# A trunk of two layers in one kernel: splits and reciprocals reordered in each layer's first up unit, loads and splits reordered at the start of the down products

## What is computed

```python
def conv_ffn(xn, buf, w_up, conv_w, conv_b, w_down):
    u = xn @ w_up
    g, v = u[..., :D_FF], u[..., D_FF:]
    gc, new_buf = causal_dwconv(g, buf, conv_w, conv_b)
    return (jax.nn.gelu(gc) * v) @ w_down, new_buf.astype(buf.dtype)
...
for layer in range(DEPTH):
    ...
    x = x + y
    f, f_i = conv_ffn(rmsnorm(x, P['f_norm'][layer]), ffn_conv[layer], P['f_w_up'][layer],
                      P['f_conv_w'][layer], P['f_conv_b'][layer], P['f_w_down'][layer])
    x = x + f
```

## Time and profile before

| | us |
|---|---|
| median of 3 runs | 2373.31 (2372.86 to 2375.99) |
| the profiled execution, its own time | 2375.29 |
| span of its trace | 2373.4 |
| TensorE busy | 2309.8 |
| VectorE busy | 1651.6 |
| ScalarE busy | 1012.8 |
| GpSimd busy | 1106.0 |
| mean granted TensorE clock | 0.987 |

### The profile page before, as it was taken

One profiled execution on the slowest core, in us unless ns is written; L12 is line 12 of the kernel. 1 busy time (PEld: TensorE's weight loads), 2 busy tenths in 40 slices (PEclk: granted clock), 3 DMA queues, 4 the chain that ended last, 5 costly groups with the idle time before them and its releaser, 6 DMA issues.

```text
span 2373.4 us, 43151 instructions
## 1 busy us (share of the span) xinstructions
PE 2309.8 (97%) x16883; PEld 2250.0 (95%) x16883; DVE 1651.6 (70%) x2170; ACT 1012.8 (43%) x1724; POOL 1106.0 (47%) x922
## 2 busy tenths in 40 slices
PE   9999997999999998999999999979999999989999
PEld 8999997999999998999999867979999999989999
DVE  7666547777777768886466675477777777788863
ACT  6555644333333334333344585443333333343331
POOL 3211454555555556556220253645555555465450
PEclk9999999999999999999999999999999999999999
DMA  4111121222222334312373203312222223243232
GB/s 132 45 45 44 61 95 52 76 81 81 81 71 65 110 115 155 110 62 96 119 108 86 65 10 107 102 50 82 81 72 64 82 81 106 84 165 112 78 101 89
DMA packets 228790, 203.04 MB, mean 86 GB/s; under 512 B 28373, under 2 KB 209821, under 8 KB 228412
## 3 DMA queue, kind: packets, MB, share of 16 engines
q1 hardware_dynamic: 224180, 188.87, 25.8%
q10 hardware_dynamic: 4404, 12.28, 2.1%
q0 software_dynamic: 64, 0.05, 0.0%
HBM read 152.41 MB, written 50.66 MB: 86 GB/s over the span
## 4 chain that ended last, share of the span: by engine, by line
PE 84%; DVE 7%; issue 4%; DMA 2%; ACT 1%; POOL 1%; SPq 0%; ACTq 0%; DVEq 0%; POOLq 0%
PE ps L1442 13%; PE ps L1441 13%; PE ps L1443 13%; PE ps L1216 9%; PE ps L1218 9%; PE ps L1217 9%; PE ps L1461 4%; PE ps L1462 4%; PE ps L1463 3%; PE ps L1676 1%; PE ps L1704 1%; PE ps L1728 1%; DVE later_slots L2944 1%; DMA part<-h_spill 1%; DVE ring L2950 1%
## 5 line engine op out<-in xcount | busy, mean ns | idle before, releaser
L1461 PE MATMUL ps<-ring,later_slots 128*128 128x272 f32 x960 | 279.6, 291 | 9.0 <-DVE later_slots L2944 9.0
L1462 PE MATMUL ps<-ring,later_slots 128*128 128x272 f32 x960 | 278.0, 290 | 0.0
L1463 PE MATMUL ps<-ring,later_slots 128*128 128x272 f32 x960 | 276.2, 288 | 0.0
L2922 DVE SCALAR_TENSOR_TENSOR y<-convin,fcol,y 128x1024 f32<-128x1024 f32 x192 | 224.4, 1209 | 18.5 <-ACT y L2147 16.8
L1441 PE MATMUL ps<-b,slot_a 128*128 128x272 f32 x768 | 221.1, 288 | 0.8 <-DVE slot_a L2876 0.8
L1442 PE MATMUL ps<-b,slot_a 128*128 128x272 f32 x768 | 221.3, 288 | 0.0
L1443 PE MATMUL ps<-b,slot_a 128*128 128x272 f32 x768 | 220.5, 287 | 0.0
L1461 PEld LDWEIGHTS ps<-ring,later_slots 128*128 128x128 f32 x960 | 182.3, 190 | 10.9 <-DVE later_slots L2944 10.8
L1462 PEld LDWEIGHTS ps<-ring,later_slots 128*128 128x128 f32 x960 | 183.0, 191 | 0.0
L1463 PEld LDWEIGHTS ps<-ring,later_slots 128*128 128x128 f32 x960 | 183.0, 191 | 0.0
L1216 PE MATMUL ps<-sa,whi 128*128 128x384 f32 (+1 forms) x540 | 178.0, 330 | 0.4 <-DVE x L2981 0.3
(11 more groups left out here) (493 smaller groups left out, 7925.0 us busy)
## 6 DMA issues: line engine op xcount, KB each, us to landing
rawu<-in_f_w_up SPq DMA_DIRECT2D x192, 256.0 KB, 4.3
h_spill<-x SPq DMA_DIRECT2D x48, 544.0 KB, 3.2
down_raw<-in_f_w_down SPq DMA_DIRECT2D x48, 384.0 KB, 4.4
part<-h_spill SPq DMA_DIRECT2D x30, 544.0 KB, 5.0
f_spill<-x ACTq DMA_DIRECT2D x16, 544.0 KB, 2.7
x<-f_spill SPq DMA_DIRECT2D x16, 544.0 KB, 7.2
raw<-in_a_w_in SPq DMA_DIRECT2D x16, 512.0 KB, 4.0
last_rows<-h_spill SPq DMA_DIRECT2D x12, 544.0 KB, 4.8
```

The lines of the kernel that those rows point to most:

```text
L1461: pe.matmul(out, slot[:, 0, i, :], b_hi, start=(i == 0 and not more), stop=False, skip_group_check=more)
L1462: pe.matmul(out, slot[:, 0, i, :], b_lo, start=False, stop=False, skip_group_check=more)
L1463: last = pe.matmul(out, slot[:, 1, i, :], b_hi, start=False, stop=(i == 2), skip_group_check=more)
L2922: ins = dve.scalar_tensor_tensor(out, g, fcol[:, u, col + t:col + t + 1], out, ALU.mult, ALU.add)
```

## The change

In the first unit of each layer: B22 and T2 are split in three rows and one as before (the piece is now called "three"), T3 and T4 in one row (2), two rows ("two") and one row (3), with row 2 of T4 and of T3 first, straight after T2's weights. Unit 1's rows are asked for when T3's row 2 is split. Reciprocal 0 moves from behind slot_b's second split to ahead of slot_c's first; reciprocal 1 moves from there to behind the last split of the unit; make_u2 moves ahead of slot_d's split and of reciprocals 1 and 2. ScalarE does slot_c's first part ahead of B22, and its third root after T4 instead of before T3. In the down products: down_raw[2] and down_raw[3] change places, stages 3 to 5 are issued before the loads of groups 2 and 3, these go half by half, and step 2's and 3's high parts wait for their first half alone. VectorE's split of B21 moves into q = 1, behind the split of the weights of step 3. The combos T3 and T4 of block 0 and B11, B21, T1 of block 1 move to later steps. No arithmetic is added or left out.

```diff
-        down_raw = [at(f"down_raw{p}", [P, 2, 3, 2, P], F32, reg_w + p * 12 * P * 4) for p in range(4)]
+        down_raw = [at(f"down_raw{p}", [P, 2, 3, 2, P], F32, reg_w + r * 12 * P * 4) for p, r in enumerate((0, 1, 3, 2))]
...
-        COMBO_ORDER += [("B11", 3), ("T1", 3), ("B22", "all"), ("B21", 3), ("B22", 3), ("T2", "all"), ("T2", 3),
-                        ("T3", "all"), ("T3", 3), ("T4", "all"), ("T4", 3)]
+        COMBO_ORDER += [("B11", 3), ("T1", 3), ("B22", "three"), ("B21", 3), ("B22", 3), ("T2", "three"), ("T2", 3),
+                        ("T4", 2), ("T3", 2), ("T3", "two"), ("T3", 3), ("T4", "two"), ("T4", 3)]
+        SPAN = {"three": 3, "two": 2}
...
                 elif u == 1:
-                    eng.wait_ge(c_lo, combo_at(layer, "T4", "all"))
+                    eng.wait_ge(c_lo, combo_at(layer, "T3", 2))
...
-                def pair_load(b, p):
...
-                        eng.wait_ge(w_lo, products_of(layer, gl) if p < 2 else ups_done(layer))
-                        eng.wait_ge(s_made, sums_of(layer, gl) if p < 2 else sums_of(layer, gl + 1))
+                        eng.wait_ge(w_lo, ups_done(layer) if p == 2 else products_of(layer, gl))
+                        eng.wait_ge(s_made, sums_of(layer, gl + 1) if p == 2 else sums_of(layer, gl))
                         if p > 0:
-                            eng.wait_ge(prod, products_of(layer, gl) + (0, 4, 6, 5)[p])
+                            eng.wait_ge(prod, products_of(layer, gl) + (0, 4, 5, 6)[p])
                     if b > 0 or p > 1:
-                        eng.wait_ge(unit_raw[p % 2], down_raw_in(layer, b, p) - 32)
+                        eng.wait_ge(unit_raw[p % 2], down_raw_in(layer, b, p) - (16 if parts == (1,) else 32))
...
-                    for e in range(2):
+                    for e in parts:
...
                 pair_load(0, 1)
-                stage(3)
-                pair_load(0, 3)
-                pair_load(0, 2)
-                stage(4)
-                stage(5)
+                for tt in range(3, FB):
+                    stage(tt)
+                for e in range(2):
+                    for p in (2, 3):
+                        pair_load(0, p, (e,))
...
-                    act.wait_ge(unit_raw[p % 2], down_raw_in(layer, b, p))
+                    act.wait_ge(unit_raw[p % 2], down_raw_in(layer, b, p) - (16 if (b, j) == (0, 0) and p > 1 else 0))
...
-                combo_hi(layer, "B22", "all")
                 weight_hi(layer, 0, 2)
+                combo_hi(layer, "B22", "three")
                 product_copy(layer, 0, 0)
                 weight_hi(layer, 0, 3)
                 scale(KD - 1)
                 combo_hi(layer, "B21", 3)
                 product_copy(layer, 0, 1)
                 combo_hi(layer, "B22", 3)
-                combo_hi(layer, "T2", "all")
+                combo_hi(layer, "T2", "three")
                 combo_hi(layer, "T2", 3)
                 weight_hi(layer, 0, 4)
+                combo_hi(layer, "T4", 2)
+                combo_hi(layer, "T3", 2)
                 root(v, 1)
-                root(v, 2)
-                combo_hi(layer, "T3", "all")
+                combo_hi(layer, "T3", "two")
                 combo_hi(layer, "T3", 3)
                 weight_hi(layer, 0, 5)
-                combo_hi(layer, "T4", "all")
+                combo_hi(layer, "T4", "two")
                 combo_hi(layer, "T4", 3)
+                root(v, 2)
                 weight_hi(layer, 0, 6)
                 weight_hi(layer, 1, 0)
...
-                    name_at = {4: "T1", 6: "B22", 11: "T2", 12: "T3", 16: "T4"}
-                    if q in name_at:
-                        down_combo_hi(layer, 0, name_at[q])
-                    elif q == 18:
-                        down_combo_hi(layer, 1, "B11")
-                    elif q < 20:
-                        pass
+                    early_ones = {4: (0, "T1"), 6: (0, "B22"), 11: (0, "T2"), 14: (0, "T3"), 18: (0, "T4"), 20: (1, "B11"),
+                                  25: (1, "B21"), 27: (1, "T1")}
+                    if q < NQ:
+                        if q in early_ones:
+                            down_combo_hi(layer, *early_ones[q])
...
-                combo_lo(layer, "B22", "all")
+                recip(v, 0)
                 weight_lo(layer, 0, 2)
+                combo_lo(layer, "B22", "three")
                 weight_lo(layer, 0, 3)
                 combo_lo(layer, "B21", 3)
                 combo_lo(layer, "B22", 3)
-                combo_lo(layer, "T2", "all")
+                combo_lo(layer, "T2", "three")
                 combo_lo(layer, "T2", 3)
                 weight_lo(layer, 0, 4)
-                recip(v, 0)
-                recip(v, 1)
-                combo_lo(layer, "T3", "all")
+                combo_lo(layer, "T4", 2)
+                combo_lo(layer, "T3", 2)
+                combo_lo(layer, "T3", "two")
                 combo_lo(layer, "T3", 3)
                 weight_lo(layer, 0, 5)
+                combo_lo(layer, "T4", "two")
+                combo_lo(layer, "T4", 3)
+                make_u2(layer, 0)
+                weight_lo(layer, 0, 6)
+                recip(v, 1)
                 seq.settle()
                 take_c11(layer, 0)
-                combo_lo(layer, "T4", "all")
-                combo_lo(layer, "T4", 3)
-                weight_lo(layer, 0, 6)
                 recip(v, 2)
-                make_u2(layer, 0)
                 seq.settle()
                 make_c12(layer, 0)
                 weight_lo(layer, 1, 0)
...
-                down_combo_lo(layer, 0, "B21")
...
-                    if q < 20:
-                        if q in (5, 7, 12, 13, 17, 19):
-                            name, to = {5: ("T1", 0), 7: ("B22", 0), 12: ("T2", 0), 13: ("T3", 0), 17: ("T4", 0),
-                                        19: ("B11", 1)}[q]
-                            down_combo_lo(layer, to, name)
-                        if q in (9, 15):
+                    early_ones = {1: (0, "B21"), 5: (0, "T1"), 7: (0, "B22"), 12: (0, "T2"), 15: (0, "T3"), 19: (0, "T4"),
+                                  21: (1, "B11"), 26: (1, "B21"), 28: (1, "T1")}
+                    if q <= NQ:
+                        if q in early_ones:
+                            down_combo_lo(layer, *early_ones[q])
+                        if q in (9, 17):
                             down_combo_make(layer, 0, "T2" if q == 9 else "T4")
```

More of the change, by code:

```diff
@@ L1471, in before @@
                     def before(cc, i):
-                        if cc == 0 and i == 0 and name in ("B22", "T2", "T3", "T4"):
-                            pe.wait_ge(c_lo, combo_at(layer, name, "all"))
+                        if cc == 0 and i == 0 and name in ("B22", "T2"):
+                            pe.wait_ge(c_lo, combo_at(layer, name, "three"))
+                        elif cc == 0 and i == 0 and name in ("T3", "T4"):
+                            pe.wait_ge(c_lo, combo_at(layer, name, "two"))
                         elif cc == 0 and i == 0 and name == "B21":
@@ L2119, in weight_hi @@
                 elif u == 0 and j == 6:
-                    act.wait_ge(c_lo, combo_at(layer, "T4", "all"))
+                    act.wait_ge(c_lo, combo_at(layer, "T4", "two"))
                 else:
```

9 lines of the change are left out of this document (5 added, 4 removed).

## The result

The changed kernel takes 2342.6 us, median of four runs (2340.2 to 2344.9), against 2373.8 (2372.9 to 2376.0) beside it: ratio 0.9867, interval 0.985 to 0.9884, so 31.2 us faster. Forecast were 2337.3 and a range of 2329 to 2351. The profiled execution took 2340.4 us with a span of 2338.2, 35.2 less than before's span.

The account below looks back on a forecast made before the run. TensorE is the path except in gaps, mostly behind VectorE's first_slots, slot_c and later_slots. First units 14.5 plus down products 23.2 make 37.7, less 1.7 gives 36.0: 2373.3 to 2337.3 us, range 2329 to 2351.

Parts of the forecast that it names:

- First unit of layer 0: Up to unit 1's product B21: finer splits and moved reciprocals start it at 401.1 instead of 407.56, gain 6.5 us.
- First unit of layer 1: Same code and waits as layer 0: 6.5 us, plus 1.5 for the half-speed stretch at 1600.4.
- Down products to step 4: Start of down products, a step being one weight group p of one product: step 4 at 898.4, gain 5.9 us.
- From step 4 on: Down products after step 4: the 5.9 us gained there counted in full in each layer's 11.6.
- The tables: Combos moved to later steps: 0.8 us of later_slots, 3.4 of two late waits, 1.5 of half-speed stretch, per layer.
- The crowding: VectorE's three-row work at steps 26 to 30: lag 2.9 us against some 3.2 of lookahead, so no cost.
- The allowance of 1.7 for new half-speed stretches: Whole kernel: 1.7 us taken off the summed gain, since remaining gaps of about 2 us may bring such stretches.
- rival 2: Crowding at steps 26 to 30 costs 3.0 us and a half-speed stretch of 1.5 per layer: 2346.3; chance 0.11.
- rival 1: Down loads: stages and p=2, p=3 halves share transfers, landing at 892 to 894; 5 us a layer lost, 2347.3; chance 0.16.
- The signs: Next trace: T3 without gap, B21 near 401, p=3's gap 2 to 3 us; wrong if later_slots keeps over 3.
- (3) More: Down products: p=3 splits without a collision and no half-speed stretch comes; 5 to 8 us better, about 2331; chance 0.08.
- (4) Late x rows: Down products: row 0 lands after 904, delaying VectorE's first take of product 1, each us costing one per layer; chance 0.03.

Follow-up runs that it names:

- e2_down: The kernel before with only the down products' part of the change (loads, stages, split of B21, step tables); 2357.9 us, ratio 0.9941.
- e5: The changed kernel with GpSimd's subtractions for down combo T3 moved behind its copy of the last unit's state, after the convolution; 2342.2 us, ratio 0.9876.
- e8: The changed kernel with splits for steps 3, 4 and B21 ahead of the convolution, last gelu and two hidden-row passes later; 2344.3 us, ratio 0.9881.
- e7: The changed kernel with VectorE's split of the second combination back ahead of the split of step 3's weights; 2343.1 us, ratio 0.9877.
- e9: The changed kernel with the last unit's convolution moved ahead of VectorE's split of step 2's weights; 2341.8 us, ratio 0.9878.
- e10: e9 with VectorE's two passes over the last hidden row at steps 6 and 8 instead of 3 and 4; 2347.8 us, ratio 0.9896.

## Why the prediction was right, and where it was off

**What bounds the kernel**: right. Only gaps and the half-speed stretches behind them were won, at the three tiles named, and in both layers.

**First unit of layer 0**, forecast 6.5, measured 6.5. In before's times unit 1's B21 starts at 401.07, forecast 401.1. Its steps held closely: T2 at 380.46 (forecast 381.05, waiting for root 2, as put), T3 without a gap, c12 starting at 391.9 (392.4), rows asked for at 380.6 (381.3), the chain from the scaling to B21 8.35 us (7.98). That the sum fits to the tenth is partly luck, since the earlier start of the chain and its greater length cancel. One thing was not in it: GpSimd's weight sum for slot_a took 1.61 us instead of 2.78. It began 0.4 us ahead of VectorE's split of B22, where before it began 0.7 us behind that start, and the split took 2.93 instead of 2.35; reciprocal 0 lay beside the sum before it (1.30 in both kernels). That the order of the two is the cause was not tested. VectorE had slot_b done 0.8 us earlier, and the wait for root 2 ate it. The loads took 6.2 us to GpSimd (6.3).

**First unit of layer 1**, forecast 8.0, measured 8.4: 6.9 to unit 1's B21, and 1.5 from the half-speed stretch at 1600.4, which is gone as put. Whether such a stretch is there to be won differs between executions: e2_down, whose first units are before's, has one behind unit 1's B21 in both layers (406.6 and 1591.1). The 6.9 does not hang on it: in the repeat of the changed kernel a half-speed stretch came at 1569.6, ahead of B21, and B21 still started 38.05 us after the unit did (38.10 in the first trace).

**Down products to step 4**, forecast 5.9, measured 3.7 and 4.2. The loads came as forecast: p=2's copy at 889.0 in before's times (landing forecast 888.6). The term that was mis-sized is the convolution, taken at 4.0 from layer 1's row; it took 6.14. In that row GpSimd's subtraction lay under the last 2.4 us alone. I had put the subtraction's start at 889.7 and the convolution's at 889.6, both from the start on, and still took the duration of the partial overlap. (889.7 is the end of GpSimd's combination before it; the prediction's words, that it starts when the stages land, don't fit its own 887.5 for them.) The difference, 2.1, and a start at 890.1 instead of 889.6 moved step 3 to 896.7 instead of 894.9, though the split behind it cost 0.54 and not 1.2. B21's split took 1.84 instead of 2.8. The gap became 4.01 instead of 2.4, and with it a stretch at half speed, so that step 3 took 3.88 us and step 4 began at 900.6 instead of 898.4, 1.6 us after its weights' split was done (890.74 + 0.56, against 892.95). After's clock, at 380, at 889 and where the earlier trace rows had 0.50:

```profile
380.40:383.80 3.40, 3.40 (x18) 3.40 (x17) 3.26 (x5) 0.63 (x1) 0.00 (x0) 0.51 0.92 265
889.00:892.40 3.40, 3.33 (x14) 3.33 (x15) 3.03 (x4) 2.63 (x5) 3.40 (x4) 0.51 1.01 408
954.00:957.40 3.40, 3.40 (x29) 3.40 (x29) 3.40 (x4) 0.77 (x2) 0.21 (x1) 1.00 0.00 0
```

**From step 4 on**, the step that failed: the forecast counted a microsecond at step 4 as one of the span. Steps 4 to 12 gave back 1.5 and 1.6 us, and the runs show the same there: 4.7 us won at step 4 by moving GpSimd's combination were worth 0.1 at step 12, and 1.7 lost at step 3 by the old split 1.0. So even the right duration for the convolution would not have brought the 5.9. What counts for step 12 is VectorE's first take of product 1. It came 21.7 us after step 0 in before and 19.8 after, and from there VectorE needs 14.7 us to the end of step 12's split in both kernels. So by this queue 1.9 us of the 3.7 could reach step 12; 2.2 did, since TensorE started 0.33 us behind that split in before and 0.05 behind it now. The forecast looked only at the first wait and not at what was late next.

**The tables**, forecast 0.8 + 3.4 + 1.5 = 5.7, measured 4.9 and 5.9 by the run with the old ones. **The crowding**, forecast nothing with a lag of 2.9 against 3.2 us, cost 0.3 and 0.9, and 0.9 in both layers of the repeat.

Down products in all: 8.4 and 8.1 instead of 11.6, 6.7 us too much for the two. The allowance of 1.7 for new half-speed stretches was needed (one came at 889 and one at 2063), and layer 1's first unit gave 0.4 more, so 4.7 of the 36.0 are missing in the places of the change, and 3.9 came from places it doesn't touch. That the gain of the profiled span (35.2) lies within 0.8 us of the forecast is luck, then; the median's gain, 31.2, is 4.8 short, and the changed kernel's four runs lie in two pairs, at 2340 and at 2345. By the time alone, 2342.6 is nearer to rival 2 (2346.3) and rival 1 (2347.3) than to the forecast of 2337.3; it is the traces that tell them apart.

**The signs.** Of what the prediction said would show it, two things did not come: step 3's gap is 4.01 us and not 2 to 3, and later_slots keeps 3.1 us (3.5 in the repeat), over the 3 that it named as a sign of being wrong. In layer 0's first block the waits on it lie at steps 10 and 12, 0.67 and 0.39 us, in the stretch where the gain was given back.

**The rivals.** (1) Transfers sharing: no; the stages were asked for at 871.5 to 872.6 and took 6.1 to 7.6 us, so they landed by 887.9 in before's times (forecast 887.5), and p=2's half when put. (2) Crowding: seen, with 0.3 and 0.9 us of the 4.5 a layer that it was priced at. (3) More: in e5 the convolution met no combination, in e8 no half-speed stretch came up to step 12 either, and neither brought anything. (4) Late x rows: the first take of product 1 ran at 905.5 in before's times without waiting for row 0; in e5, where the row was late, the take waited 1.59 us for it, as the rival's mechanism has it, and the time stayed where it was.

## What to carry to other kernels

Reordering pays where TensorE waits for one operation behind others that nobody waits for yet: three reciprocals, a reload held by a counter two splits too late. Before counting a microsecond at a gap, follow the engine that feeds it through the next ten steps, and ask whether the change brings the start of its unbroken queue nearer or puts work into it; here, where VectorE and GpSimd were busy for 90% and 80% of the stretch and VectorE had no gap in the last 14.7 us, a gap closed was a gap moved. For an operation that may overlap another engine's, take the duration from a row with the same overlap, or count both ends.

## What the hardware did that was not expected

How much the two engines slow each other depends on the overlap. The convolution, four instructions with two SBUF inputs, took 2.99 to 3.00 us with GpSimd idle, 3.85 with it busy for 1.1 us of that, 4.07 for 2.4, 5.17 for 3.6 (layer 1 of e7), 6.14 for 4.9, and 6.44 in e9, where GpSimd was busy under all of it. In the changed kernel the subtraction under it took 5.09 us, and the one of the same shape just before it, with the convolution not yet begun, 3.99. From the start of the one to the end of the other (882.18 to 888.55) the two took 6.4 us, where 3.0 and 4.0 one after the other would make 7.0: side by side saved 0.6 us. The Trainium skill (SBUF — State Buffer, Who interferes with whom) says that such an instruction contends and one with at most one SBUF input doesn't. The trace agrees with both: GpSimd's two sums beside a reciprocal took 1.31 and 1.29, and the shortest of that form in the trace take 1.28.

A stretch at 1.2 GHz came behind nearly every TensorE gap of 3 us or more in these stages (at 380, 889, 1554 and 2063 in the changed kernel), but more of them lie in the attention stage, which no kernel here changed, and their length varies. Behind a gap of 2 us it came in some executions and not in others: not behind the 2.04 us at 392.11 in the changed kernel, but at 394.7 in e10 behind the same gap. From the last down matmul of layer 0 to the first unit of layer 1 the profiled runs took 458.6 to 459.7 us with 6.8 us at half speed (nine of them), 461.1 with 10.2, 462.4 with 13.7 (before) and 463.8 and 464.0 with 17.1. That is 2.7 of the 35.2 us of the span, and a spread of 5 us that belongs to no edit: as much as the two pairs of the changed kernel's runs lie apart. That these pairs have this cause is likely and not shown, since each run but the profiled one left only its time and mean clock (0.994 and 0.993 for the pair at 2340, 0.993 and 0.992 for the one at 2345). The start of layer 0's first unit, ahead of everything that was edited, varies too, from 361.6 to 363.4 us.
